# Weight casts ahead of the first norms: one in place of three, with two behind the second and two behind the third root

## The reference

```python
def layer(x, ...):
    xn = rmsnorm(x, g_pre_mix)
    z = xn @ w_in                                  # 1024 -> 6144
    xa, ga, u, v, gates = jnp.split(z, [D_RNN, 2 * D_RNN, 2 * D_RNN + D_GMLP, 2 * D_RNN + 2 * D_GMLP], axis=-1)
    xc, conv_new = causal_conv(xa, conv_prev, conv_w, conv_b)
    hseq, h_last = rglru(xc, h0, w_a, b_a, w_x, b_x, lam)      # gates by matmul, then a scan over time
    o_a = (hseq * jax.nn.gelu(ga)) @ w_br_a
    vn = layernorm(jax.nn.gelu(v), ln_g, ln_b)
    o_b = (jax.nn.gelu(u) * spatial_gate(vn, w_s, b_s)) @ w_br_b
    g_a, g_b = jnp.split(jax.nn.sigmoid(gates), 2, axis=-1)
    x = x + rmsnorm((g_a * o_a + g_b * o_b) @ w_out, g_post_mix)
    hn = rmsnorm(x, g_pre_ffn)
    gate, up = jnp.split(hn @ w_ffn_in, 2, axis=-1)
    return x + rmsnorm((jax.nn.silu(gate) * up) @ w_ffn_out, g_post_ffn), h_last, conv_new, vn
```

## Time and profile before

| | us |
|---|---|
| median of 3 runs | 2074.46 |
| lowest and highest | 2071.74, 2078.29 |
| the profiled execution, as timed | 2075.16 |
| its span (first to last instruction of the slowest core, 5) | 2073.6 |
| spans of the other cores | 2064.5 to 2071.8 |

### The profile page before, as it was taken

One profiled execution on the slowest core, in us unless ns is written; L12 is line 12 of the kernel. 1 busy time (PEld: TensorE's weight loads), 2 busy tenths in 40 slices (PEclk: granted clock), 3 DMA queues, 4 the chain that ended last, 5 costly groups with the idle time before them and its releaser, 6 DMA issues.

```text
span 2073.6 us, 34614 instructions; the slowest of 8 cores (2064.5 to 2073.6 us)
## 1 busy us (share of the span) xinstructions
PE 2041.6 (98%) x10690; PEld 1012.4 (49%) x10690; DVE 1190.3 (57%) x1815; ACT 913.3 (44%) x1541; POOL 401.5 (19%) x816
## 2 busy tenths in 40 slices
PE   8999999999999999999999999999999999999998
PEld 3444444444444444444454455445565555455554
DVE  5889388525784267733665168624872687335243
ACT  5588476124651256412761157314742473133111
POOL 4323343112220122101210032002200321121000
PEclk9999999999999999999999999999999999999999
DMA  9965789997389865676655476447666746775662
GB/s 204 187 160 92 193 182 220 192 230 238 128 198 215 224 228 147 178 205 214 210 183 164 149 260 210 156 154 239 213 217 211 242 147 206 228 255 183 198 203 82
DMA packets 113671, 401.42 MB, mean 194 GB/s; under 512 B 14089, under 2 KB 14097, under 8 KB 113490
## 3 DMA queue, kind: packets, MB, share of 16 engines
q1 hardware_dynamic: 96786, 340.43, 49.7%
q0 software_dynamic: 16272, 57.68, 17.4%
q10 hardware_dynamic: 432, 1.09, 0.2%
HBM read 403.26 MB, written 53.54 MB: 220 GB/s over the span
## 4 chain that ended last, share of the span: by engine, by line
PE 93%; DMA 3%; ACT 1%; DVE 1%; issue 1%; POOL 0%; SPq 0%; DVEq 0%; ACTq 0%; POOLq 0%
PE ps L789 64%; PE ps L1385 14%; PE ps L1283 5%; PE ps L1079 5%; DMA xin<-xp 2%; PE ps L970 1%; PE ps L685 1%; PE ps L1398 1%; PE ps L1142 1%; DVE xcf L952 1%; DMA wring<-wall 1%; DMA x<-xp 1%; ACT ffT L679 0%; DVE xcf L948 0%; ACT ffT L1239 0%
## 5 line engine op out<-in xcount | busy, mean ns | idle before, releaser
L789 PE MATMUL ps<-xnT,wring 128*128 128x512 bf16 (+2 forms) x5696 | 1154.3, 359 | 4.1 <-ACT xnT L874 1.0
L789 PEld LDWEIGHTS ps<-xnT,wring 128*128 128x128 bf16 x5696 | 553.5, 98 | 551.0 <-issue 14.4
L1385 PE MATMUL ps<-wring,ffT 128*128 128x512 bf16 x1364 | 296.0, 379 | 0.0
L1364 ACT ACTIVATE sgt<-ps 128x512 f32<-128x512 f32 (+2 forms) x198 | 109.4, 555 | 409.1 <-PE ps L789 377.7
L1368 DVE SCALAR_TENSOR_TENSOR sgt<-sgt,ps 128x512 f32<-128x512 f32 (+2 forms) x198 | 125.3, 633 | 194.1 <-PE ps L789 191.8
L1385 PEld LDWEIGHTS ps<-wring,ffT 128*128 128x128 bf16 x1364 | 133.4, 98 | 160.8 <-issue 0.5
L952 DVE SCALAR_TENSOR_TENSOR xcf<-xa,vecs_sb,xcf 128x512 f32<-128x512 f32 (+2 forms) x240 | 164.9, 687 | 26.3 <-DVE xcf L952 0.9
L1370 DVE SCALAR_TENSOR_TENSOR ffT<-sgt,ps 128x512 bf16<-128x512 f32 (+2 forms) x198 | 125.9, 636 | 40.4 <-PE ps L789 36.5
L657 POOL TENSOR_SCALAR stats<-stats 128x1 f32<-128x1 f32 (+1 forms) x132 | 37.5, 284 | 460.1 <-ACT ffT L670 372.4
L501 POOL DMA_DIRECT2D wring<-wall x113 | 62.9, 557 | 319.7 <-PE ps L789 206.8
L1408 ACT ACTIVATE sgt<-ps 128x512 f32<-128x512 f32 x66 | 38.6, 594 | 194.5 <-PE ps L1385 182.8
(11 more groups left out here) (167 smaller groups left out, 2102.7 us busy)
## 6 DMA issues: line engine op xcount, KB each, us to landing
wring<-wsc SPq DMA_DIRECT2D x473, 512.0 KB, 4.5
wring<-wall POOLq DMA_DIRECT2D x107, 512.0 KB, 11.0
wsc<-wring SPq DMA_DIRECT2D x68, 512.0 KB, 8.7
x<-xp SPq DMA_DIRECT2D x31, 512.0 KB, 7.2
yp<-x SPq DMA_DIRECT2D x29, 512.0 KB, 6.9
xin<-xp SPq DMA_DIRECT2D x28, 512.0 KB, 6.5
wring<-wsc SPq DMA_DIRECT2D x12, 256.0 KB, 3.0
wring<-wall POOLq DMA_DIRECT2D x6, 256.0 KB, 6.8
```

What stands on the lines that cost most here:

```text
L789: mm(lambda e, k=k: e.matmul(ps[:, b, 0:nt], lhsT=wv[:, k, m * 128:(m + 1) * 128], rhs=rhsT[:, k, 0:nt], start=(k == 0), stop=(k == NCH - ...
L1364: act(lambda e: e.activation(out=sgt[:, i, 0:nt], in_=ps[:, b, 0:nt], func=AF.Tanh, scale=0.5), nt, [("ps", b)], [("sgt", i)])
L1385: mm(lambda e, j=j, kk=kk, b=b, PT=PT, col=col: e.matmul(ps[:, b, :], lhsT=ffT[:, j, col:col + 128], rhs=wv[:, kk, :], start=(j == 0), sto ...
```

## The change

The change touches one line, the ladder of `most`. The first step, which holds until the second row block's `xsq` is emitted, is 1 instead of 3. A new step of 3 holds from there until the third row block's `xsq` is emitted. The steps 5 (until the fourth) and 8 stay: 5 now begins behind the third row block's `xsq`, where it began behind the second's.

```diff
@@ -510,7 +510,7 @@
                 if dry:
                     return
                 at = P.free["pe"]
-                most = 0 if ("su_zero",) not in done else 3 if ("xsq", 0, 1) not in done else 5 if ("xsq", 0, 3) not in done else 8 if ("xsq", 1, 3) not in done else len(stream)
+                most = 0 if ("su_zero",) not in done else 1 if ("xsq", 0, 1) not in done else 3 if ("xsq", 0, 2) not in done else 5 if ("xsq", 0, 3) not in done else 8 if ("xsq", 1, 3) not in done else len(stream)
                 while wo and P.ready([("wr", wo[0])]) <= at and ("xl", 1, 3) in done:
                     copy_back(wo.popleft())
```

## The result

The changed kernel takes 2081.96 us (median of 7 runs) against 2074.46 us for the kernel before. The ratio is 1.0038, with a 95% interval of 1.0024 to 1.0051. That is 7.9 us slower (5.0 to 10.6 us). The forecast, no change, was wrong; the time lies inside the stated range and on the side of rival C. The slowest run of each kernel, 2490.83 us and 2187.80 us, was disturbed and is left out of the ratio.

A forecast was written before the change was run, and what follows sets the result against it. TensorE, busy for 98% of the span, was taken as the bound, so only its waits or low clock could pay. Terms 0 - 0.3 + 0 + 0 + 0 = -0.3 us on the 2074.5 us median gave 2074 us, range 2065 to 2085 us.

The forecast's parts named there:

- rival C: Second tile's norm late for TensorE near 42 us, plus a 5.5 us late load from the new order: 2085 us; chance 0.24.
- Part 1: Head, POOL: two casts fewer ahead of the norms; the 1.2 us were hidden by the load of x, gain 0.
- Part 2: Head, DMA engines: two casts fewer queued might let x land earlier; bounds 0 and 0.7 us, taken as 0.3 us gain.
- rival A: Head: x does land earlier, up to 1.5 us off the first projection, 2073 us; chance 0.10.
- Part 3: Head, POOL: two casts behind the third root fit the room before the fourth block; cost 0 to 1.16 us, taken as 0.
- Part 4: Cast queue runs dry near 14.5 us for 0.4 us, hidden by 0.66 us margin at the second tile's transposes; cost 0.
- far bound: Cast queue near 14 us: slow start as in the head, 5.6 us from issue, data at 17.6 us, gap 3.1 us.
- Part 5: Whole kernel: the planner rewrites the order behind the head; bounds -8 and +11 us, taken as 0.
- B: Stretch at 77 us: new order loses the cast wait and low clock there, and half the late ScalarE waits; 2066.6 us; chance 0.22.

The follow-up runs named there:

- e1: Kernel before with its order of all engines, but the first eight casts on POOL grouped as in the changed kernel (1, 2, 2, 3); ratio 0.9999 to before.
- e2: Changed kernel with its new order, but the first eight casts on POOL grouped as before (3, 2, 0, 3); ratio 1.0040 to before.
- e6: Kernel before, without the wait for the wsS copy at L1142 in all tiles but the last; ratio 1.0004 to before.
- e10: Kernel before with its casts, only the planner's account of TensorE set 263 ns later at the first projection, giving another order; ratio 1.0019 to before.
- e7: Kernel before with its order, but one cast first and the other seven behind the fourth root; ratio 1.0028 to before.
- e3: Changed kernel with one ScalarE pair pinned as before (GELU of the third block's first half behind the second tile's first square); ratio 1.0023 to before.
- e0: The changed kernel measured again with no edit; 2083.68 us, ratio 1.0045 to the kernel before.
- e4: Changed kernel, without the wait for the wsS copy at L1142 in all tiles but the last; ratio 1.0019 to before.
- e8: Changed kernel without the wsS copy wait, second tile's transposes 1 and 3 moved into the v group ahead, seven warming matmuls removed; ratio 1.0017 to before.
- e9: Changed kernel with the wsS copy wait kept, second tile's transposes 1 and 3 moved into the v group ahead, seven warming matmuls removed; ratio 1.0079 to before.

## Why the prediction was wrong

**Part 1** (two casts fewer on POOL, 0): right. POOL was idle for 4.12 us in that place, 3.52 before; the 0.6 us more (and not 1.2, as the squares were summed 0.5 us earlier) return nothing.

**Part 2** (x lands earlier, 0.3 us): the reason was right, the gain absent. To 14 us the cast queue of after had moved 129 packets on core 5, 128 before, so the two casts had moved nothing by then in either kernel.

The first projection came at 21.0 us on the mean instead of 20.8, and in e1 at 20.8. The arrival of the fourth block moves more from execution to execution than the edit could move it: on core 3 its square starts at 16.83 us in after and 15.23 us in before, on core 7 at 11.97 and 14.51 us. More executions say the same: over the four profiled with the old casts (before, e2, e6, e10) the first projection starts at 20.4 us on the mean, over the nine with the new casts (e7 left out) at 20.7 us, each with a spread of 0.6 us or more. No gain shows, and rival A is out.

**Part 3** (casts behind the third root, 0): right. On core 5 the pair ends at 14.78 us and the fourth block's sum starts 1.87 us later. The rule of the Trainium skill that was weighed there (page "SBUF — State Buffer", on SWDGE) gave 0.8 us more; the pair at 13.62 us took 1.16 us like the one at 11.48 us. That is no test of the rule: line 676, on which the prediction had put it, starts at 15.22 us on this core, 0.4 us behind the end of the pair, and what VectorE ran beside the pair was line 690, another kind of operation. No run here shows the rule at work or refuted for this pair.

**Part 4** (the queue runs dry for 0.4 us, hidden by a margin of 0.66 us): the mechanism is there, its size was a little too small, the margin was misread, and it cost 0.4 us in e1. DMA share in the stretches of 14 to 15 us, core 3, before and then after (length, busy PE, PEld, DVE, ACT, POOL, clock, DMA share, GB/s):

```profile
14.00:15.00 1.00, 1.00 (x9) 0.72 (x8) 0.18 (x1) 0.00 (x0) 0.00 (x0) 0.50 1.00 172
```

```profile
13.00:14.00 1.00, 0.00 (x0) 0.00 (x0) 0.82 (x1) 0.94 (x1) 0.79 (x3) 0.50 0.71 139
14.00:15.00 1.00, 0.92 (x9) 0.95 (x10) 0.00 (x0) 0.00 (x0) 1.00 (x2) 0.50 0.62 102
```

The margin first. The prediction took it from the end of the scaling (41.46 us) to the transposes (42.12 us). But the transposes also wait for a GELU that stands behind the scaling in ScalarE's queue (line 1092), and in before its row on core 5 is the first of these three; the other two are the same pair on core 0:

```profile
41.37 0.58 ACT L1092 ACTIVATE x<-ps 128x512 f32<-128x512 f32 x1
...
40.51 0.58 ACT L1092 ACTIVATE x<-ps 128x512 f32<-128x512 f32 x1
...
41.23 0.61 PE L685 MATMUL ps<-identb,ffT 128*128 128x128 bf16 x8 [0.68 <-ACT x L1092]
```

On core 0, where TensorE did wait, the transposes start 0.14 us behind the end of the GELU; on core 5 they start 0.17 us behind it. So core 5 had 0.03 us to spare and not 0.66, and core 0 already waited 0.7 us and core 2 1.4 us in before.

The second tile's loads went out 1.0 us later on the mean (28.6 us; 27.6 before), and on core 5 at 29.48 us:

```profile
29.48 0.94 SPq L848 DMA_DIRECT2D xin<-xp  x2
...
44.25 0.61 PE L685 MATMUL ps<-identb,ffT 128*128 128x128 bf16 x8 [1.69 <-ACT x L1092]
```

So on core 5 the wait that rival C named is there in after, 1.69 us, and on five other cores too. With the order of before a delay of 0.9 us (e1) left 0.2 to 1.4 us of wait, 0.7 us on the mean against 0.3 in before, and the milestone 0.4 us later. In the sum of part 4 the far bound is off by 0.1 us (10 - 4.31 is 5.7 us, not 5.6), which changes nothing.

**Part 5** (the order, taken as 0): this is the step that failed. I wrote that some stages would change places and that nothing named a side, and I put bounds of -8 and +11 us on it. The measured effect of the order is e2's: +0.40%, 8.3 us. That it lies inside the bounds is luck, as they were read from stretches that had no part in it. Two things in the trace of before named a side, and I didn't read them. First, in the order of before each of the second tile's four transposes is covered by 16 matmuls, with not a wait from 22 to 74 us on core 3 (one of 0.7 and 1.4 us on cores 0 and 2); in such a stretch a change of order has much more to lose than to win. My bounds came from 100 us on. Of the new order's loss only the nine warming matmuls at 333 us lie there, 2.1 us, and the waits from 110 to 290 us even fell by 1.5 us on the mean. Second, the waiter at 69.13 us had its copy 0.5 us ahead.

A third thing needs no trace. The planner's accounts can be read when the program is recorded, and they name the side: the third tile's first L1283 stands 6.5 us later in the account of after than in that of before, and so does the end. The first one stands 4.3 us later, 1.7 us of it the eight matmuls that changed sides. Measured were 6.4 and 7.4 us at the third tile. For e3 the account says 3.1 us and the execution 3.1. It is no full price: it has the copy land 1.2 us ahead of its waiter in after, where the chip lost 2.0 us, and for e10 it says 2.9 us, where the profiled execution was ahead of before. Taking part 5 as 0 "as nothing names a side" was therefore the wrong step, and not only an unlucky one.

The sum of what the traces show, in means over the cores, up to the third tile's first L1283: 0.4 us at the head (first L1079 at 31.5 against 31.1 us; in e0 it comes at 30.7, so this part is chance), 3.9 us of warming matmuls (1.8 in the two stretches, 2.1 at 333 us), and 2.6 us more of waits between 22 and 290 us (4.5 us in before, 7.0 in after). In these 2.6 us are 2.0 for the copy, 1.6 for line 690 and 0.8 more for the GELU at the first transposes; 0.6 for the cast at 77 us and 1.2 of others went away. Between 290 and 700 us the waits are equal (2.3 and 2.2 us). That is 6.9 us where 6.4 were measured.

**The rivals.** C had the sign and nearly the time (2085 us) by luck, as the mechanism is another: not mainly the late loads, and no late stretch of 5.5 us behind 100 us. Its wait at 42 us came true on six of eight cores, but it is 0.8 us more than in before on the mean, an eighth of the loss. B named the wait at 77 us for a cast. On core 3 this wait of 1.2 us is gone in after, as B wanted, but no part of a gain is left of it: TensorE's clock still fell, the share is 0.94 in both kernels. The rows of core 3, before and after:

```profile
70.00:100.00 30.00, 28.36 (x142) 13.38 (x141) 24.57 (x40) 16.69 (x24) 4.92 (x14) 0.94 0.96 219
```

```profile
70.00:100.00 30.00, 25.70 (x122) 11.58 (x121) 20.48 (x34) 22.46 (x32) 6.56 (x19) 0.94 1.01 219
```

The wait for the copy has taken its place, at 74 us, and the 2.66 us less of busy time in these 30 us are most of the 3.84 us of the wait.

**Open.** The ratio of e4 and e8, 1.0019 and 1.0017, is about 4 us; rows name the two stretches and the nine warming matmuls at 333 us for it, but no experiment took either away. e10's time is not explained. How much the casts cost under the new order (0 to 2.6 us by the milestones of e2) was not settled. Only the pair of 79 ns was tested as a turning point; what else the planner turned was not.

## What to carry to other kernels

Where a planner writes the order, an edit of one line is two edits. Split them, the old order with the new placement and the new order with the old one, before reasoning about the placement: here the part that the edit was about cost 0.4 us at most by the milestone, which the ratio can't tell from nothing, and the order 8 us. Read the planner's own account of the end before and after the edit: it was 6.5 us later here. Look in the old profile for stretches with no wait at all and for waiters whose data landed just in time, as these set the side on which a reshuffle comes out. And a condition that covers a cell which the instruction doesn't read is free until an order moves its producer; then it cost 2 to 4 us, and 8 to 11 us in e9.

## What the runs showed of the hardware

- **A 16 KB copy has no landing time of its own.** From issue to landing it took 4.0 to 6.1 us in before, 2.1 to 7.7 us in after (2.1 us on cores 1 and 5, issued at 66.9 and 66.2 us) and 10.7 to 13.8 us in e9, where it was issued between two 512 KB casts. On core 5 it goes out 0.28 us ahead of the first cast in after (2.1 us) and 0.92 us behind it in e9 (10.7 us); on core 3 of after it is also 0.28 us ahead and takes 7.6 us. What sets the time was not separated.
- **The first cast of the head starts slowly.** Issued at 4.31 us, it had moved 1 packet by 10 us before and 3 by 10 us in after, with two casts fewer queued behind it; into an idle queue at 49.47 us data came 2.9 us behind the issue. The x loads, issued ahead of it, were under way at the time; that they are the cause was not tested.
- **A short dry stretch of the cast queue did little harm here.** In e1 the DMA share fell to 0.49 on core 1 and 0.64 on core 7 between 13 and 14 us (1.03 in before on both), the milestone came 0.4 us later, and the time was 0.9999 of before. In e7, where the share was 0.00 to 0.02 between 15 and 16 us on all cores, the time was 1.0028.
